# Down blocks of the last feed-forward as seven products of halves, and packed input and forget columns

## The reference, cut to what matters

```
def swiglu(h, w_gate, w_up, w_down):
    return (jax.nn.silu(h @ w_gate) * (h @ w_up)) @ w_down
...
# second_block, D_FF = 2816
    xin = h @ w_in                      # 8 of its columns are ig and fg
    log_i = (ig + b_igate)              # input gate, 4 heads
    log_f = jax.nn.log_sigmoid((fg + b_fgate))
...
    h = modulate(rms_norm(x, g_ffn[l]), sh_f, sc_f)
    x = x + gt_f[:, None, :] * swiglu(h, w_gate[l], w_up[l], w_down[l])
```

## Time and profile before

| | us |
|---|---|
| median of 3 runs | 2034.1 (2034.06 to 2034.44) |
| the profiled execution | 2034.22 |
| its span, first to last instruction | 2032.4 |
| TensorE busy | 2026.5 |
| VectorE, ScalarE, GpSimd busy | 1220.5, 894.1, 1038.9 |

### The profile page before, as it was taken

One profiled execution on the slowest core, in us unless ns is written; L12 is line 12 of the kernel. 1 busy time (PEld: TensorE's weight loads), 2 busy tenths in 40 slices (PEclk: granted clock), 3 DMA queues, 4 the chain that ended last, 5 costly groups with the idle time before them and its releaser, 6 DMA issues.

```text
span 2032.4 us, 29841 instructions
## 1 busy us (share of the span) xinstructions
PE 2026.5 (100%) x10896; PEld 1712.4 (84%) x10896; DVE 1220.5 (60%) x2142; ACT 894.1 (44%) x1361; POOL 1038.9 (51%) x773
## 2 busy tenths in 40 slices
PE   9999999999999999999999999999999999999999
PEld 7788778889889878877788899898877788989898
DVE  5677335576757637854356767567445478647363
ACT  4124353536446422244445355364446544536352
POOL 5454334476555754443355755556343334656555
PEclk9999999999999999999999999999999999999999
DMA  6332212343543343321233443433221212233233
GB/s 223 107 104 84 83 63 101 117 166 105 187 147 124 104 130 101 104 83 64 82 111 128 142 151 144 166 104 104 97 85 66 80 42 104 84 104 105 104 104 104
DMA packets 37492, 223.99 MB, mean 110 GB/s; under 512 B 6012, under 2 KB 6524, under 8 KB 11744
## 3 DMA queue, kind: packets, MB, share of 16 engines
q1 hardware_dynamic: 31424, 193.48, 27.7%
q10 hardware_dynamic: 5920, 28.55, 4.1%
HBM read 215.59 MB, written 2.10 MB: 107 GB/s over the span
## 4 chain that ended last, share of the span: by engine, by line
PE 98%; DVE 1%; DVEq 0%; issue 0%; ACT 0%; ACTq 0%
PE ps L599 18%; PE ps L601 18%; PE ps L600 18%; PE ps L756 6%; PE ps L758 6%; PE ps L757 6%; PE ps L616 4%; PE ps L617 4%; PE ps L618 4%; PE ps L684 2%; PE ps L648 1%; PE ps L650 1%; PE ps L649 1%; PE ps L705 1%; PE ps L694 1%; PE ps L726 0%
## 5 line engine op out<-in xcount | busy, mean ns | idle before, releaser
L519 POOL TENSOR_TENSOR w_lo<-w_raw,w_hi 128x512 fp32r<-128x512 f32 x544 | 732.0, 1377 | 775.8 <-ACT w_hi L1168 766.5
L1168 ACT ACTIVATE w_hi<-w_raw 128x2048 fp32r<-128x2048 f32 x134 | 256.1, 1911 | 383.5 <-PE ps L601 290.7
L599 PE MATMUL ps<-a_hi,w_hi 128*128 128x512 f32 (+1 forms) x888 | 352.2, 397 | 0.0
L601 PE MATMUL ps<-a_hi,w_lo 128*128 128x512 f32 (+1 forms) x888 | 346.2, 390 | 0.0
L600 PE MATMUL ps<-a_lo,w_hi 128*128 128x512 f32 (+1 forms) x888 | 345.8, 389 | 0.0
L533 POOL TENSOR_TENSOR w_lo<-w_raw,w_hi 128x512 fp32r<-128x512 f32 x164 | 214.6, 1331 | 160.9 <-ACT w_hi L1295 160.9
L599 PE MATMUL ps<-b_hi,w_hi 128*128 128x512 f32 x612 | 238.1, 389 | 0.0
L600 PE MATMUL ps<-b_lo,w_hi 128*128 128x512 f32 x612 | 238.1, 389 | 0.0
L601 PE MATMUL ps<-b_hi,w_lo 128*128 128x512 f32 x612 | 238.1, 389 | 0.0
L599 PEld LDWEIGHTS ps<-a_hi,w_hi 128*128 128x128 f32 (+1 forms) x888 | 165.3, 186 | 48.0 <-issue 9.7
L601 PEld LDWEIGHTS ps<-a_hi,w_lo 128*128 128x128 f32 (+1 forms) x888 | 165.3, 186 | 36.8
(11 more groups left out here) (394 smaller groups left out, 4523.6 us busy)
## 6 DMA issues: line engine op xcount, KB each, us to landing
w_raw<-in_weights SPq DMA_DIRECT2D x176, 1024.0 KB, 4.9
v<-in_ada ACTq DMA_DIRECT2D x24, 1024.0 KB, 4.9
out<-x SPq DMA_DIRECT2D x8, 256.0 KB, 2.5
x<-in_x_in SPq DMA_DIRECT2D x3, 512.0 KB, 6.8
w_raw<-in_weights SPq DMA_DIRECT2D x4, 256.0 KB, 5.5
yc<-in_c_rows ACTq DMA_DIRECT2D x2, 512.0 KB, 3.2
bias<-in_mult_bias ACTq DMA_DIRECT2D x1, 640.0 KB
x<-in_x_in SPq DMA_DIRECT2D x2, 256.0 KB, 4.7
```

What stands on the lines that cost most here:

```text
L519: nc.gpsimd.tensor_tensor(w_lo[:, s, piece], w_raw[:, s, piece], f32(w_hi[:, s, piece]), ALU.subtract).then_inc(w_lo_ready, 1)
L599: nc.tensor.matmul(o, wh, hi(kt), start=kt == 0, stop=False)
L601: last = nc.tensor.matmul(o, wl, hi(kt), start=False, stop=kt == depth - 1)
L1168: nc.scalar.activation(w_hi[:, n % 2, :], w_raw[:, n % 2, :], ACT.Copy).then_inc(w_hi_ready, 1)
```

## The change

**Fast down blocks.** `FAST` takes in the down blocks but the first of each part, and in part 3 but the last too: 28, 29, 30, 40, 41, 42, 50, 51. `fast_block` gets its source, its sums and its depth as arguments; in part 3 a half has 3 slices, so that a product is 9 matmuls and a block 63. The hidden slices are laid out so that the second half starts at slot 4 (`h_slot`), and the rows of `w_down` in the same way. The sums of quadrants of the hidden layer are new work: VectorE forms them pair by pair behind each up block (`h_forms`), and at the first down block ScalarE makes their high parts (`h_sum_high`) and VectorE their low parts (`h_sum_low`). The fourth of them goes over the quadrant of `b_hi` and `b_lo` that it is formed from, behind the first down block. What a fast down block gives is added to x from `sums` (SBUF), and not from PSUM.

**Scratch.** The scratch for dynamic DMA shrinks from 16 KB to 1 KB of each partition; the room holds the new buffers (`hs`, `hs_raw`, `late_raw`), and all tensors lie lower.

**Gates.** The weights of the eight gate columns (block `C_IF`) stand twice in the block, 100 columns in place of 36. The second copy is overwritten with its own low part (`split_gates`, one instruction on GpSimd in place of four), so that one matmul gives both high and low: 16 matmuls in place of 24, and VectorE adds the two results, two instructions more.

```
-FAST = [j for j, kind, *_ in feed_forward() if kind != "down" and j >= C_FF + 5]
+def fast_kind(j, kind, hid, b, nt):
+
+    if kind == "down":
+        return 0 < b - nt < (3 if nt == FF_TILES[-1] else 4)
+    return j >= C_FF + 5
+
+
+FIRST_DOWNS = [j for j, kind, hid, b, nt in feed_forward() if b == nt]
+FAST = [plan[0] for plan in feed_forward() if fast_kind(*plan)]
...
+            def split_gates(n, s):
+                pool.wait_ge(w_hi_ready, n - 1)
+                raw, hi = (m[:, s, :].rearrange("p (k c) -> p k c", k=KT)[:, :, LOW_ROW:IF_ROWS] for m in (w_raw, w_hi))
+                nc.gpsimd.tensor_tensor(hi, raw, f32(hi), ALU.subtract).then_inc(w_lo_ready, 4)
...
+            def gate_rows(t, s):
...
+                for kt in range(KT):
+                    for part in (a_hi, a_lo):
+                        last = nc.tensor.matmul(ps[t % 4][0:IF_ROWS, :], wcols(w_hi, s, KT, kt, 0, IF_ROWS), part[:, kt, :],
+                                                start=kt == 0 and part is a_hi, stop=kt == KT - 1 and part is a_lo)
...
+                    if j in FAST:
+                        fast_block(L, FF, FAST.index(j), j, FAST_USES[j], (b_hi, b_lo), h_sums[part_], nt // 2,
+                                   lambda i: pe.wait_ge(ht_split, 4 * part_ + T_ORDER.index(i) + 1))
...
                 column_high(f, 0).then_inc(w_hi_ready, 1)
+                if j in FIRST_DOWNS:
+                    for i in T_ORDER[0:3]:
+                        h_sum_high(FIRST_DOWNS.index(j), i)
...
+            def h_sum_high(part_, i):
+
+                act.wait_ge(ht_raw, 4 * part_ + T_ORDER.index(i) + 1)
+                deep = FF_TILES[part_] // 2
+                nc.scalar.activation(h_sums[part_][i][0][:, 0:deep, :], h_sums_f32[i][:, 0:deep, :], ACT.Copy).then_inc(ht_hi, 1)
...
+                if j in FIRST_DOWNS and u == 1:
+                    h_sum_high(FIRST_DOWNS.index(j), T_ORDER[3])
...
+                def h_forms(n):
+
+                    far, i = divmod(n, nt // 2)
+                    t1, t2, t3, t4 = (m[:, i, :] for m in h_sums_f32)
+                    left, right = g[:, 6 + n % 2, 0:HS], g[:, 6 + n % 2, HS:S]
+                    if far == 0:
+                        tt(t1, left, right, ALU.subtract)
+                        nc.vector.tensor_copy(t3, right)
+                        return
+                    nc.vector.scalar_tensor_tensor(t2, right, -1.0, t1, ALU.mult, ALU.subtract)
+                    tt(t3, right, t3, ALU.subtract)
+                    dve.drain()
+                    nc.vector.scalar_tensor_tensor(t4, left, -1.0, t2, ALU.mult, ALU.subtract)
...
                 if j + 1 in FAST:
                     sum_low(L, FF, FAST.index(j + 1), 1)
+                if j in FIRST_DOWNS:
+                    h_sum_low(1)
+                    h_sum_low(0)
...
                 if j + 1 in FAST:
                     sum_low(L, FF, FAST.index(j + 1), 2)
+                if j in FIRST_DOWNS:
+                    h_sum_low(2)
...
                     for u in range(2):
                         h_low(hid + b - 1 + u)
-                    dve.drain()
+                    for u in range(2):
+                        h_forms(b - 1 + u)
+                    if j + 1 in FIRST_DOWNS:
+                        dve.drain().then_inc(ht_raw, 4)
+                    else:
+                        dve.drain()
...
+                if j in FIRST_DOWNS:
+                    h_sum_low(3)
...
-    nc = bacc.Bacc("TRN2", target_bir_lowering=False, num_devices=1)
+    nc = bacc.Bacc("TRN2", target_bir_lowering=False, num_devices=1, dynamic_dma_scratch_size=DMA_SCRATCH)
```

More of the change, by code:

```diff
@@ L203, in two_blocks @@
         ctx.enter_context(one)
+        thirteen = ExitStack()
+        hs = [sb(f"hs{i}", [P, 2, HK, HS], F32R, thirteen) for i in range(2)]
+        thirteen.close()
+        hs_raw = sb("hs_raw", [P, 2, 2, HK * HS])
         four = ExitStack()
@@ L590, in low_parts, with product @@
                 return low
-            def product(o, s, deep, depth, c0, m, hi, lo, low, tiles=1, between=None, at=5):
-                for kt in range(depth):
+            def product(o, s, deep, depth, c0, m, hi, lo, low, tiles=1, between=None, at=5, slots=None):
+                slots = slots or range(depth)
+                for kt in slots:
                     low(kt, deep)
@@ L754, in part @@
                     (fh, fl), (mh, ml) = form, moving
-                    for kt in range(HK):
+                    for kt in range(depth):
                         nc.tensor.matmul(o, fh[:, kt, :], mh[:, kt, :], start=kt == 0, stop=False)
                         nc.tensor.matmul(o, fh[:, kt, :], ml[:, kt, :], start=False, stop=False)
-                        last = nc.tensor.matmul(o, fl[:, kt, :], mh[:, kt, :], start=False, stop=kt == HK - 1)
+                        last = nc.tensor.matmul(o, fl[:, kt, :], mh[:, kt, :], start=False, stop=kt == depth - 1)
                     return last
@@ L1031, in _ @@
                         if u == 0:
-                            tile(L, t, s, KT, 0, a_hi, a_lo, low, m=F_ROW + MH, tiles=2)
+                            gate_rows(t, s)
                     elif j > 1:
@@ L1125, in _ @@
             j, hid = C_FF, 0
-            for nt in FF_TILES:
+            for part_, nt in enumerate(FF_TILES):
+                slots = [h_slot(n, nt) for n in range(nt)]
                 for b in range(nt):
@@ L2625 @@
             parts += [blocks(a[m][0][:, at + P * i:at + P * i + 256]) for m in ("w_gate_2", "w_up_2")]
-        parts += [blocks(a["w_down_2"][0][at:at + P * nt])]
+        rows = np.zeros((D, D), w.dtype)
+        for n in range(nt):
+            rows[P * h_slot(n, nt):P * h_slot(n, nt) + P] = a["w_down_2"][0][at + P * n:at + P * n + P]
+        parts += [blocks(rows)]
         at += P * nt
```

103 lines of the change are left out of this document (70 added, 33 removed).

## The result

| | before | after |
|---|---|---|
| median of 6 runs | 2034.1 us (2034.1 to 2034.4) | 2080.7 us (2079.5 to 2082.4) |
| ratio | | 1.0229 [1.0216, 1.0242] |
| profiled execution, its span | 2034.2, 2032.4 | 2079.5, 2077.7 |
| granted TensorE clock, mean | 1.000 | 0.988 |

The change costs 46.6 us. The forecast was 2082.0, between 2055 and 2091, slower.

What follows compares the result with a forecast made beforehand. TensorE's work was taken to bound the kernel, provided other engines keep ahead. From 2034.2 us, minus 7.8 of gains, plus 47.1 of stalls and 8.4 of clock gave 2081.9, so 2082; range 2055 to 2091.

Steps and rivals of the forecast that it cites:

- Gains: Matmuls removed from fast down blocks and gate columns save 7.8 us: 6.0 and 1.8; scratch counted as nothing.
- First down blocks: TensorE waits at blocks 28, 40, 50 for bank 0, freed by VectorE's addition to x: 35.3 us in sum.
- Block 39's chain: VectorE's list from block 39's start frees bank 0 at 21.9 us; TensorE stands from 10.9, so 11.0 us.
- First fast blocks: Forms ahead of weight sums delay TensorE at block 24 by 4.6 us and block 26 by 5.0 us.
- nothing is to spare: Block 26's second product already waits for bank 1, so block 24's forms add their whole 5.0 us.
- Steady blocks: Forms make bank 1 late behind far, near and mixed pairs in later gate blocks: 2.2 us in sum.
- Clock: Slower TensorE clock behind the three long stalls costs 8.4 us; nothing for the two of 5 us.
- The value from the start of the program: Slow matmuls after idleness at program start, taken as 2.8 us lost behind each long stall.
- (a): TensorE's clock holds behind the stalls: 2073.5 us; chance 18%.
- (b): GpSimd and VectorE miss each other by luck of phase: 2051.6 us, 2060.0 with the clock; chance 14%.
- (c): First down blocks do not stall on bank 0: 2026.4 us, plus 5 us at most; chance 6%.
- (d): Fast down blocks show pitches other than 0.120 us; at 0.130 the saving is gone; no separate chance given.

Runs made afterwards that it cites:

- stalls: Kernel before with three waits of TensorE put in by hand ahead of blocks 28, 40 and 50 (about 5, 11, 11 us planned); 2068.5 us.
- pool_wait: Kernel after, with GpSimd's first two quadrant subtractions of each fast block waiting until VectorE's forms are done; 2064.2 us.
- late_forms: Kernel after with a second down block of each part plain and up-block forms moved later, mostly into the following gate block; 2055.1 us.
- banks: Kernel after with the first down blocks' results in banks 2 and 3, not 0 and 1; 2069.0 us.
- both: Kernel after with GpSimd's first quadrants waiting for the forms and, in first down blocks, additions to x ahead of the sums' low parts; 2050.7 us.

## Why the forecast held, term by term

The sum was 2081.9, measured were 2080.7 in the median and 2079.5 in the profiled execution. It held by its mechanism: the waits stand where they were forecast and are ended by what was named. That it held to within 2.4 us is partly luck, because errors in its terms offset each other: against the forecast, gains took off 0.6 us more, the first down blocks cost 2.0 and block 26 2.4 less, and the steady blocks cost 1.8 and the clock 0.6 more.

**Gains, 7.8 forecast, 8.4 measured.** The fast down blocks gave their 0.80 and 0.60 us exactly; blocks at full clock last 10.08 and 7.56. The gate rows give 2.1 by their own run, not 1.8: the row priced the matmuls rightly, and a wait that I had not connected with them became some 0.3 us shorter; the other 0.3 of the 2.4 us up to block 19 are within the scatter of its start. The scratch gives nothing, as said.

**First down blocks, 35.3 forecast, 33.3 measured (10.0, 11.0, 12.3).** Block 39's chain, counted from the block's start as the forecast did (forecast in brackets): low parts of the hidden tiles at 5.0 (4.0), forms at 9.4 (9.1), `sum_low` at 14.6 (14.4), third low part of the sums at 21.3 (21.1), bank 0 at 21.9 (21.9). The end is right because two steps cancel: the multiplications ahead of the low parts ran into GpSimd and took 2.56 us for two, while the forms took 4.5 and not 5.0. For block 27 the forecast read from the trace of before that the low parts end a microsecond later than at 39. They ended a microsecond earlier in the kernel after (1.50 us for its two multiplications, which had been 2.57), and with that the wait was 10.0, a microsecond below block 39's and not one above it. Which engine meets which is not a property of a block; it changes once anything upstream shifts.

**First fast blocks.** Block 24: 4.7 us more wait, 4.6 forecast, though by other halves: the near pair behind 20 took 2.3 us and the one behind 22 took 3.5, for 1.5 and 3.8. Block 26: 2.6 for 5.0. The failed step is "nothing is to spare". In the trace of before VectorE was behind in block 25: its multiplications for block 24 began 4.3 us into it. The wait in block 24 let VectorE catch up; they began 2.4 us into block 25, which with forms of 4.5 us makes 5.0 - 1.9 - 0.5 = 2.6. I had added two waits of which the first pays into the second.

**Steady blocks, 2.2 forecast, 4.0 measured.** By the lengths of the blocks: behind the near pairs 0.6 at block 36 and nothing at 34 and 46, for 0.15 each; behind the far pair 2.1 at block 38 for 1.1; behind the mixed one 1.2 at block 48 for 0.6. The mechanism is the forecast one, its size was put at half.

**Clock, 8.4 forecast, 9.0 measured.** Here the size was right and the split was wrong: the three long waits cost 5.7 us and not 8.4, and those at blocks 24 and 26, which I had put at nothing, 3.3; the three of under 2 us cost none. The value from the start of the program, 2.8 us for a wait, was at the upper end of what was measured: 1.4, 2.7 and 1.6 here, 1.5, 1.4 and 2.3 in stalls. What I had not seen is that a wait of 3 to 5 us can cost as much as one of 11.

**The rivals.** (a) a clock that holds: out, by the windows and by stalls. (b) no collisions, 2051.6 to 2060.0: out for this kernel, but pool_wait shows that the order of the lists decides it. Even then the long waits stay, at 8 to 9 us and not at 6 to 7, since the low parts of 1024 columns still meet GpSimd. (c) the first down blocks do not stall, and (d) another pitch: out.

What stays open: what sets how long the lower clock lasts behind a wait. By the lengths of the blocks, every wait of over 4 us in these traces cost something (1.1 to 2.7 us), none of under 1.9 us did, and of those between some cost 1.3 to 1.7 us and some nothing (2.8 us at block 41 of late_forms, 3.6 at block 26 of banks). Of the 2.4 us that both moves together gave beyond their sum, the part in block 24 is such a case; the rest is not explained.

## What to carry to other kernels

A change that takes matmuls away and gives the other engines more to do is judged at the block in which their new work falls together with a handover: follow the list of the engine that frees the next bank, instruction by instruction, to the instruction that frees it. Here 6 us of matmuls were bought with some 45 us of waiting. The same trade paid, with 1.6 us, only in part 2, with one more plain block between the preparation and its use, with GpSimd held back during the forms and an addition to `x` moved ahead of the low parts; in part 3, whose blocks are shorter, it did not pay even so. Where a full TensorE is made to wait for more than 4 us, add 1 to 3 us of clock for each wait; a wait of 2 to 4 us may cost 1.5 or nothing. And first look at whether VectorE's SBUF work and GpSimd's can be kept apart: one semaphore was worth 16.5 us.

## What the runs showed of the hardware

A single wait of TensorE of 4.6 us cost 1.5 us of clock behind it, one of 10.8 us cost 1.4 (kernel stalls); even behind 2.8 us of waiting at block 26 of the kernel after 1.4 us were lost. Two waits of 2.9 and 2.8 us in one execution (late_forms, blocks 29 and 41) cost 1.5 us and nothing, and two of 2.1 and 2.0 us at block 24 of pool_wait and of both cost 1.3 and nothing. An operation of VectorE on 256 columns of SBUF took 0.42 us alone and 1.35 to 1.51 beside GpSimd's subtraction of 512 columns, a copy 0.28 and 1.38: small as it is, it was over only behind GpSimd's running instruction (1.27 us alone). GpSimd loses far less in return, 2.94 for 2.56 us over two instructions.
